# Two blocks on one core: where the second attention's latents are split, which of its values come first, and whether the last projection keeps its split weights

## The reference

```python
def second_block(x, positions, w_in, q_norm_g, w_uq, kv_norm_g, w_ukv, pool_w, pool_scale, w_out, ln_g, ln_b):
    alpha = (2.0 * DEPTH) ** 0.25
    h = x @ w_in
    x_q, x_kv, k_rope_raw, gate_a, u_pool, gate_b = jnp.split(h, splits, axis=-1)   # 512, 256, 64, 512, 512, 512
    y_a = mla_branch(x_q, x_kv, k_rope_raw, positions, q_norm_g, w_uq, kv_norm_g, w_ukv) * jax.nn.silu(gate_a)
    y_b = pool_branch(u_pool, pool_w, pool_scale) * jax.nn.silu(gate_b)
    mix = jnp.concatenate([y_a, y_b], axis=-1) @ w_out
    return layer_norm(alpha * x + mix, ln_g, ln_b)

def mla_branch(...):        # 4 heads, no causal limit in the work done: every block of 128 queries sees 1024 keys
    q = (rms_norm(x_q, q_norm_g) @ w_uq)                # 128 plain and 64 rotated columns a head
    kv = (rms_norm(x_kv, kv_norm_g) @ w_ukv)            # 128 key and 128 value columns a head
    # rope on q_rope and k_rope_raw, softmax(q k^T * scale, masked by position) @ v, in blocks of 128 queries
```

## Time and profile before

| | |
|---|---|
| median of 3 runs | 2448.18 us (2445.73 to 2453.65) |
| profiled execution | 2448.01 us |
| its span, first to last instruction | 2446.2 us |
| PE busy in the span | 2338.3 us (96%) |
| DVE, ACT, POOL busy | 1545.6, 781.1, 1145.2 us |
| input units of the second block end | 2057 us |
| attention, first logits to last values | 2153.9 to 2317.6 us |
| last projection | 2322.1 to 2425.5 us |

### The profile page before, as it was taken

How to read it: one execution, slowest core, us unless ns; L and a number is a source line. 1 busy time by engine, 2 the same in 40 slices (tenths; PEclk the granted TensorE clock), 3 DMA queues, 4 the chain that set the end, 5 groups by cost and what they waited for, 6 DMA issues and landing times. The chain is left out here.

```text
span 2446.2 us, 30442 instructions
## 1 busy us (share of the span) xinstructions
PE 2338.3 (96%) x11310; PEld 1931.9 (79%) x11310; DVE 1545.6 (63%) x1925; ACT 781.1 (32%) x1038; POOL 1145.2 (47%) x917
## 2 busy tenths in 40 slices
PE   7999999999999999999999999999999999899995
PEld 5678877888888898887778888788888877689874
DVE  7899999955556354445666667777777002434478
ACT  4311232133322356113333334334431122244413
POOL 4136523333222346433388888989864322200164
PEclk9999999999999999999999999999999999899998
DMA  4021224532222413444144445644412110411122
GB/s 153 31 85 61 77 86 129 163 119 92 100 95 87 129 36 118 137 133 155 69 174 163 146 143 219 232 159 152 147 44 82 43 43 22 146 48 40 49 77 95
DMA packets 97713, 261.51 MB, mean 107 GB/s; under 512 B 8304, under 2 KB 32120, under 8 KB 92600
## 3 DMA queue, kind: packets, MB, share of 16 engines
q1 hardware_dynamic: 79376, 192.77, 23.1%
q10 hardware_dynamic: 18216, 67.13, 7.9%
HBM read 183.57 MB, written 77.61 MB: 107 GB/s over the span
## 5 line engine op out<-in xcount | busy, mean ns | idle before, releaser
L998 PE MATMUL pair<-actA,w_hi 128*128 128x512 f32 x2048 | 638.0, 393 | 4.3 <-ACT stage L1532 2.3
L851 POOL TENSOR_TENSOR pad<-pad 128x1 f32<-128x1 f32 x142 | 39.2, 276 | 1059.4 <-PE pair L998 753.6
L998 PEld LDWEIGHTS pair<-actA,w_hi 128*128 128x128 f32 x2048 | 383.1, 188 | 88.1 <-issue 4.5
L998 PE MATMUL pair<-actA,w_lo 128*128 128x512 f32 x1024 | 399.3, 390 | 0.0
L855 POOL TENSOR_TENSOR w_lo<-raw,w_hi 128x1024 fp32r<-128x1024 f32 (+2 forms) x142 | 318.0, 2240 | 11.4
L1332 PE MATMUL pair<-tring,wsp 128*128 128x512 f32 x1344 | 308.4, 392 | 6.0 <-DVE tring L2529 5.7
L1332 PEld LDWEIGHTS pair<-tring,wsp 128*128 128x128 f32 x1344 | 254.1, 189 | 60.2 <-issue 6.5
L998 PEld LDWEIGHTS pair<-actA,w_lo 128*128 128x128 f32 x1024 | 192.6, 188 | 40.6
L1332 PE MATMUL pair<-tsp,wsp 128*128 128x512 f32 x768 | 184.5, 392 | 7.9 <-DVE u_c L2504 4.0
L2497 DVE TENSOR_TENSOR xB<-pair,xB 128x1024 f32<-128x1024 f32 x112 | 136.3, 1219 | 72.9 <-PE pair L1332 72.8
L998 PE MATMUL pair<-actB,w_hi 128*128 128x512 f32 x576 | 178.1, 390 | 0.0
(11 more groups left out here) (344 smaller groups left out, 4204.8 us busy)
## 6 DMA issues: line engine op xcount, KB each, us to landing
raw<-w_in SPq DMA_DIRECT2D x80, 512.0 KB, 3.3
wraw<-w_pair SPq DMA_DIRECT2D x32, 1024.0 KB, 7.1
staged<-hid_d SPq DMA_DIRECT2D x56, 512.0 KB, 3.3
proj<-stage ACTq DMA_DIRECT2D x40, 512.0 KB, 2.6
hid_d<-hsum SPq DMA_DIRECT2D x16, 1024.0 KB, 5.0
gates<-proj ACTq DMA_DIRECT2D x24, 512.0 KB, 5.3
raw<-w_out SPq DMA_DIRECT2D x24, 512.0 KB, 3.3
hid_d<-hid SPq DMA_DIRECT2D x16, 512.0 KB, 2.8
```

What stands on the lines that cost most here:

```text
L851: nc.gpsimd.tensor_tensor(pad[:, 0:1], pad[:, 1:2], pad[:, 1:2], ALU.add)
L998: last = nc.tensor.matmul(pair[par][:, cols], w[:, par, wk], x[:, cols], start=(k == 0 and i == 0), stop=(k == kt - 1 and i == 2))
```

## The change

Six edits, all in the second block:

1. ACT parks the residual `xB` in DRAM (`x_d`, two DMAs of 2 MB) after input unit 1; SP loads it back after it has issued the queries of attention block 2. Its 32 KB (and 112 to 120) hold six buffers for squares (`sq6`) and then the hi parts of the latents meanwhile. `xq_lo` takes 56 to 72 KB.
2. ACT squares x_q after input unit 13 and x_kv after unit 14; PE makes both means of squares after unit 15; ACT's roots and hi copies and DVE's norms and lo parts come before ACT reads units 16 and 17.
3. `swap(2)` (kr) follows the first unit of `w_uq`, `swap(0)` and `swap(1)` the second and the third; the rotary work of DVE and ACT moves forward with them. The four DMAs of the rotary queries are issued between the third and the fourth plain query unit.
4. The value heads come first in `w_ukv`, the key heads after them, and between key heads PE transposes the values and ACT copies them. The wait of attention for `k2` is per head.
5. The last projection has its own activation buffer `actC`, half by half: half 0's hi parts are made by ACT around its last two softmax steps, the lo parts by DVE between its last attention steps; half 1's follow the attention. Eight split weights are kept (`w_hi`/`w_lo`, `w_kept`, `w_last`), split once; half 1 splits none. Four half-wide PSUM banks take the products in turn in place of two.
6. POOL no longer centres and scales tiles 6 and 7 of half 1; DVE does all eight.

ACT's list between the second plain query unit and the key heads, before: `q2st` is a plain query head's buffer, `q_d` and `qr_d` DRAM, `k` the key heads.

The diff, cut:

```diff
-        xqS = at("xqS", 120, [P, 2, 4, S], F32R)
-        xkvS = at("xkvS", 152, [P, 2, 2, S], F32R)
-        tmp2 = at("tmp2", 168, [P, 2, S])
+        sq6 = at("sq6", 88, [P, 6, S])
+        xq_hi = at("xq_hi", 88, [P, 4, S], F32R)
+        xq_lo = at("xq_lo", 56, [P, 4, S], F32R)
+        xkv_hi = at("xkv_hi", 104, [P, 2, S], F32R)
+        xkv_lo = at("xkv_lo", 112, [P, 2, S], F32R)
+        rstd_kv = at("rstd_kv", 80, [P, S])
...
-        q2st = at("q2st", 56, [P, 2, 2, S], F32R)
+        q2st = at("q2st", 152, [P, 2, 2, S], F32R)
...
+        actC = at("actC", 120, [P, 2, NT, 2, HALF], F32R)
+        w_kept = [at(f"w_kept{j}", kb, [P, 2, 1024], F32R) for j, kb in enumerate((56, 64, 72, 80, 48))]
+        w_last = [at("w_last0", 195.5, [P, 1024], F32R), at("w_last1", 203.5, [P, 1024], F32R)]
...
+        def product_bank(c):
+            n = FIRST["out2"] + c
+            col = (c // 2) % 2 * HALF
+            return pair[n % 2][:, col:col + HALF]
...
             for b in range(NB):
                 load_q2(b)
+                if b == 2:
+                    sp.dma_start(xB[:, 0:4, :], x_d[:, 0:4, :]).then_inc(xB_back, 16)
+                    sp.dma_start(xB[:, 4:8, :], x_d[:, 4:8, :]).then_inc(xB_back, 16)
             load_units("w_out2", FIRST["out2"], NT, 8)
-            load_units("w_out2", FIRST["out2"] + NT, NT, 8)
...
-            split_units(FIRST["out2"], N_OUT2, 8)
...
+            for j in range(NT):
+                n = FIRST["out2"] + j
+                hi, lo = kept(j)
+                pool.wait_ge(w_in[n % 2], (n // 2 + 1) * 16)
+                if j < 2:
+                    pool.wait_ge(unit_mm, n - 1)
+                if j == 2:
+                    pool.wait_ge(unit_mm, FIRST["out2"] + 1)
+                if j == 6:
+                    pool.wait_ge(lo_ok, 4 * NT + 10 + 2 * NT)
+                nc.gpsimd.tensor_copy(hi, raw[:, n % 2, :]).then_inc(w_hi_ok, 1)
+                pool.wait_ge(w_hi_ok, n + 1)
+                nc.gpsimd.tensor_tensor(lo, raw[:, n % 2, :], hi.bitcast(F32), ALU.subtract).then_inc(w_split, 1)
...
+            product(n + 1, (n + 1) % 2, (n + 1) // 2, 8, hB, lB)
             stat("xq", "mean512", 4)
-            products(FIRST["in2"] + 15, 4, 8, hB, lB)
+            stat("xkv", "mean256", 2)
+            for n in range(FIRST["in2"] + 16, FIRST["in2"] + N_IN2):
+                product(n, n % 2, n // 2, 8, hB, lB)
...
-            stat("xkv", "mean256", 2)
...
+            swap(2)
             for u in range(1, N_UQ):
                 n = FIRST["uq"] + u
                 product(n, n % 2, n // 2, 4, qh, ql)
-                if u == 3:
-                    swap(0)
-                    swap(1)
-                if u == 4:
-                    swap(2)
+                if u <= 2:
+                    swap(u - 1)
             pe.wait_ge(lo_ok, base + 6)
-            products(FIRST["ukv"], N_UKV, 2, lambda k: xkvS[:, 0, k, :], lambda k: xkvS[:, 1, k, :])
...
+            for u in range(N_UKV):
+                n = FIRST["ukv"] + u
+                product(n, n % 2, n // 2, 2, lambda k: xkv_hi[:, k, :], lambda k: xkv_lo[:, k, :])
+                if u >= 4:
+                    unit_read(pe, n - 4)
+                    transposes(("v2T", u - 4), lambda c: v4[:, u - 4, c * P:(c + 1) * P], NB)
...
+                pe.wait_ge(unit_out[n % 2], n // 2 - (c >= 2))
...
+                if n == FIRST["in2"] + 2:
+                    for j in (0, 4):
+                        act.dma_start(x_d[:, j:j + 4, :], xB[:, j:j + 4, :]).then_inc(xB_out, 16)
...
                 nc.scalar.copy(q2st[:, h % 2, 0, :], pair[n % 2][:, :]).then_inc(q2_hi, 1)
                 n += 1
+                if h < 3:
+                    rope_hi(h)
                 if h >= 1:
                     park_q2(h - 1)
...
+                if h == 2:
+                    act.wait_ge(r_lo, 3)
                     for s in range(2):
                         rows = slice(s * 64, s * 64 + 64)
                         act.dma_start(qr_d[0:64, s::2, :], qr_hi[rows, :, :].bitcast(F32)).then_inc(qr_parked, 16)
                         act.dma_start(qr_d[64:128, s::2, :], qr_lo[rows, :, :].bitcast(F32)).then_inc(qr_parked, 16)
...
+            def first_half(i):
+                if i == N2 - 1:
+                    wait_ready(act, ("qk", 1, N2 - 1))
+                    branch_half(0, range(4))
+
+            attention(1, MLA_HEADS, at2, 0, first_half)
+            branch_half(0, range(4, NT))
             for b in (NB - 2, NB - 1):
                 wait_done(act, ("yT", 1, b))
+            branch_half(1, range(NT))
...
+            def first_half(i):
+                if i == N2:
+                    low_half(0, range(4))
+                if i == N2 + 2:
+                    low_half(0, range(4, NT))
+
+            attention(1, MLA_HEADS, P, float(192) ** -0.5, at2, 0, 0, mask2, gated, first_half)
             for b in (NB - 2, NB - 1):
                 wait_done(dve, ("yT", 1, b))
+            low_half(1, range(NT))
+            dve.wait_ge(xB_back, 32)
...
-            centre(1, mine[0:1])
+            centre(1, range(1))
             variance(1)
-            centre(1, mine[1:])
-            scale(1, mine)
+            centre(1, range(1, NT))
+            scale(1, range(NT))
```

More of the change, by code:

```diff
@@ L1428, in half_product @@
             def half_product(j, half):
[L1429 to L1439 removed]
+                c = half * NT + j
+                n, out = FIRST["out2"] + c, product_bank(c)
+                whi, wlo = kept(j)
+                if half == 0:
+                    pe.wait_ge(w_split, n + 1)
+                pe.wait_ge(unit_out[n % 2], n // 2 - (c >= 2))
+                for k in range(NT):
+                    if j == 0:
+                        pe.wait_ge(lo_ok, base + 6 + half * NT + k + 1)
+                    wk, xh, xl = slice(k * P, (k + 1) * P), actC[:, half, k, 0, :], actC[:, half, k, 1, :]
+                    for i, (w, x) in enumerate(((whi, xh), (whi, xl), (wlo, xh))):
+                        mm = nc.tensor.matmul(out, w[:, wk], x, start=(k == 0 and i == 0),
+                                              stop=(k == NT - 1 and i == 2))
                 mm.then_inc(unit_mm, 1)
@@ L1759, in _, with attention @@
                     square(STAT_BASE[("hg", h)], mpair(key)[:, :])
-            def attention(st, heads, buf, i0):
+            def attention(st, heads, buf, i0, beside=None):
                 N = NB * heads
                 for i in range(N + 1):
+                    if beside:
+                        beside(i)
                     if i < N:
@@ L2043, in finish @@
                 for j in tiles:
-                    if half and j in BY_POOL:
-                        act.wait_ge(scaled_pool, BY_POOL.index(j) + 1)
-                    else:
-                        act.wait_ge(scaled, NT * half + j - sum(x < j for x in BY_POOL if half) + 1)
+                    act.wait_ge(scaled, NT * half + j + 1)
                     nc.scalar.activation(xB[:, j, cols], xB[:, j, cols], ACT.Identity, bias=SM("ln_b", j),
@@ L2304, in _, with attention @@
             finish(HG_HEADS - 1)
-            def attention(st, heads, dv, scale, buf, i0, b0, mask, write):
+            def attention(st, heads, dv, scale, buf, i0, b0, mask, write, beside=None):
                 N = NB * heads
                 for i in range(N + 4):
+                    if beside:
+                        beside(i)
                     if i < N:
@@ L2718, in move @@
                 if j < 2:
-                    V.scalar_tensor_tensor(x, x, float(2.0 ** 0.25), pair[par][:, 0:HALF], ALU.mult, ALU.add) \
+                    V.scalar_tensor_tensor(x, x, float(2.0 ** 0.25), product, ALU.mult, ALU.add) \
                      .then_inc(unit_out[par], 1)
@@ L2722, in move @@
                     dve.wait_ge(lessened, half * (NT - 2) + j - 1)
-                    V.tensor_tensor(x, pair[par][:, 0:HALF], x, ALU.add).then_inc(unit_out[par], 1)
+                    V.tensor_tensor(x, product, x, ALU.add).then_inc(unit_out[par], 1)
                 dve.wait_ge(unit_out[par], n // 2 + 1)
@@ L2753, in gather_sq @@
                     V.tensor_tensor(sq_sum[:, cols], sq_sum[:, cols], sqh[:, c % 2, :], ALU.add).then_inc(dev_sum, 1)
-            mine = [j for j in range(NT) if j not in BY_POOL]
             def keep_mean(half):
@@ L2783, in gather_both @@
                 gather_sq(c)
-            move(0)
-            dve.wait_ge(lo_ok, base + NT)
+            dve.wait_ge(lo_ok, base + 2 * NT)
             for half in range(2):
                 c = half * NT
-                if half:
-                    move(c)
+                move(c)
                 move(c + 1)
```

173 lines of the change are left out of this document (83 added, 90 removed).

## The result

The changed kernel takes 2412.14 us (median of 4 runs, 2409.43 to 2413.58) against 2448.61 us of the kernel before, measured beside it: ratio 0.9848, 95% interval 0.9828 to 0.9867. Run again later it gave 2406.68 us (5 runs, 2405.63 to 2412.67), ratio 0.9831 (0.9817 to 0.9846). The forecast was 2412 us. The profiled execution took 2413.39 us, its span 2411.5, at a mean clock of 0.986.

What follows compares the result with a forecast made beforehand. PE bounds the kernel, busy 96% of the span, its late waits on DVE and ACT, never a DMA. Savings of 24.5 (to attention), 9.4 (last projection) and 2.4 (tail) sum to 36.3 us off 2448.01: 2412 us, range 2402 to 2422.

Steps and rivals of the forecast that it cites:

- signs of being wrong: Attention beginning later than 2135, PE waiting for `xB` in half 1, or block 3's queries landing late.
- Latents: Before `w_uq`: roots, norms, splits covered by three input units (32.7 us); first unit at 2058.4, no wait; parking and reload cost 0.
- Head units: `w_uq` to second value head: old waits go; ACT's four DMA issues (5.55 us) leave a 4.3 us wait plus 2.9 clock.
- Values first: Value and key heads: seven heads 19.0 us, transposes 4.0, nothing waits; attention starts at 2129.3, 24.5 us less.
- End of attention: Last attention steps: ACT's half-wide copies add 0.65 us; first half product at 2319.3, not 2322.11.
- First mean: After two half products: four DVE rests alternate with POOL's splits, 9.3 us; PE waits 4.9 us plus 2.9 of clock.
- Half 1: Last projection, second half: no split beside it, DVE's 30 to 34 us just hidden under 34 of PE, no waits.
- Tail: After the last product: DVE's seven centrings alone take 4.3 us, against five in 6.70 beside POOL; 2.4 us less.
- less waiting: Rival: DMA issues cost ACT little, or DVE isn't held before the first mean; 6 or 8 us less, 2404 to 2406; chance 0.2.
- the queue did not back up more: Rival, ACT's queue: rotary DMAs all at 2.41 us, 4 us, and 4 more before first value copy; 2416 to 2420; chance 0.17.
- DVE did not bound half 1: Rival, last projection: DVE's late start or waits add 3 to 10 us at the last product; 2415 to 2424; chance 0.1.
- block 3's queries: Slower rival: SP's 4 MB reload delays these queries and attention waits; 2457 if landing takes 85 us; chance 0.02.

Runs made afterwards that it cites:

- e9: The kernel before, run and profiled once more without any edit: first part 1998.55 us, 450.55 us behind the pooling.
- e5: Changed kernel with ACT's rotary-query DMAs and parks spread among the value reads: pooling to first logits 131.15 us against 133.33.
- e6: Changed kernel with POOL repeating eight weight splits beside half 1, in buffers nobody reads: tail 9.4 us longer, 10.6 in all behind the pooling.
- e7: Changed kernel with the half products in two PSUM banks, each waiting for the second before it: +4.3 us up to the last product.
- e4: Changed kernel with means of squares, roots and copies behind the last input unit, without cover: median 2414.95 us; middle 9.95 us longer.
- e1: Changed kernel with the four rotary-query DMAs issued by SP among its w_ukv loads instead of by ACT: 2414.76 us (4 runs).
- e11: Changed kernel with POOL's splits of reloaded branch halves two logits later in the first attention: median 2402.74 us, first part 1988.53 us.
- e8: Changed kernel with both POOL's repeated splits beside half 1 and two PSUM banks: 108.44 us to the last product, 15.1 us longer behind the pooling.
- e3: Changed kernel with POOL again centring and scaling tiles 6 and 7 of the last half: median 2409.55 us, tail 20.25 us, 2.45 more.

## Why the prediction was right, and where it was not

The time was met and the mechanisms were those forecast, but that it was met to a fraction of a microsecond is luck, since two errors cancel: the four parts gave 43.6 us and not 36.3, and the first window took 8.9 us back in the same execution. The second error is not the change's: e9 shows the long first window in the kernel before, and e5, e6 and e7 the short one with the change in. The 7.3 us of the first error lie in the middle (3.1), in attention and last projection together (3.6) and in the tail (0.5). The second profiles of both kernels (450.55 and 409.67 us behind the pooling) give 40.9 for the four parts. All runs of the two kernels together say 2448.69 (median of 48 runs) and 2410.62 (9 runs), 38.1 us.

One of the forecast's own signs of being wrong came: attention begins at 2135.11, later than 2135. It isn't the head units' doing, which are 3.1 us shorter than forecast, but the first window's 8.9 us; the sign was set in absolute time, as if that window were fixed. A slip of the forecast on which nothing rests: the 124 us left "from its last transposes" are counted from the first half product, and from the transposes they are 128.1.

- *Latents*: forecast was the first `w_uq` matmul 4.1 us sooner; it came 4.5 sooner (69.64 against 65.13 us behind the cut), without a wait. That the cover does it: e4. The parking cost nothing: 147.71 us from ACT's read of the first input unit to the cut with it and without, and its two DMAs lie in this stretch. Nobody waits for the reload; neither was tested by itself.
- *Head units*: the wait stood at the place forecast, behind the work forecast (5.6 us of issues for 5.55). It was 3.4 us, not 4.3. The step that failed is "first query head is parked at 2087.6": the DMA's issue has the start of the copy that stands two places ahead of it in ACT's list (2094.17 both, which is 2085.7 in the forecast's time), so the third head's copy never waited for the park. And of 2.9 us of clock behind the gap only some 1.5 came (0.71 in five us), worth less than that: in e6 and e7 the same 3.38 us gap kept full clock, PE then waited 0.6 to 0.7 us for ACT one head later, and the middle was only 0.3 to 0.4 us shorter. From first `w_uq` matmul to first logits 68.2 us, not 70.9. Together the middle gave 27.7 us for 24.5.
- *Values first*: no wait at any of seven units, as forecast. Edits 3 and 4 were not run apart, so which of them took away the old waits for the key heads (6.9 us) is argued and not shown.
- *End of attention*: +0.69 us for +0.65; first product 0.41 us behind the last transposes for 0.5. No run has the new last projection with the old late splits, so the price of the old 3.4 us wait for the first operand is read from the two timelines alone.
- *First mean*: the hold came turn and turn about, as forecast from the 2.83 us row, but the last four rests stood behind three operations of POOL and not four, 6.38 us for 9.3, since the first of them got in as POOL's first began. Wait 1.84 for 4.9. The 2.9 us of clock didn't come in this profile, but 1.6 to 1.9 came in e1, e6, e7 and e11. Last product 93.66 us behind the transposes for 97.2. That is 3.5 us less where wait and clock are 6.0 less; part of the difference is a term mis-sized the other way, the three means between the halves, 2.5 us (2357.99 to 2360.49) for the 1.3 forecast.
- *Half 1*: without waits, as forecast; why before had them: e6 to e8.
- *Tail*: 2.9 for 2.4; e3 shows 2.45 of it, the other half a microsecond I did not trace.
- *Rivals*: "less waiting" is what the profile behind the pooling shows (some 7 us more), hidden by the first window; the queue did not back up more; DVE did not bound half 1; block 3's queries were issued at 2168.86 behind the reload and nobody waited for them.

What was missing is a term for the clock's chance: I took a gap's price (2.9 us for 4.93) from one row as a fixed sum, and the untouched three quarters of the span as fixed too. In e9 the same gap cost 1.2 us less.

## What to carry to other kernels

Cut both spans at shared events before crediting a change: the parts showed 2.45 us in the tail where the medians had the other sign. A row of DMAs in an engine's list is worth its issue time to the first instruction behind it, and moving it gains only what its new queue doesn't hold back: 5.0 us lost behind SP, 2.2 won when spread. More PSUM banks let PE run ahead of a slow engine, but most of the delay then comes where the backlog must be gone: 10.3 us of waits at the products with two banks (e8), 9.5 behind the last product with four (e6).

## What the runs showed that I had not expected

- The clock behind a gap of PE is not a function of the gap alone: 1.86 to 1.99 us at one place kept full clock in four profiles and lost it in two; 1.84 or 1.85 us at the first mean kept it in six profiles (among them both of the changed kernel) and lost it in four (e1, e6, e7 and e11, 0.66 in five us each); 3.38 us at the second value head kept it in e6 and e7 and lost it in the others that have it (0.66 to 0.72). The Trainium skill, "TensorE: Matmul & The Clock Gate", "Part 1: The HAM clock gate (the "warmup" mystery)", calls the number of matmuls at the lower clock run-variable at a kernel's start; these rows show the same late in a long one: with the same gap PE runs at the lower clock in some executions and not in others.
- A reload that came 1.2 us late in the first attention was followed by 6.2 us of loss on PE; but e9 is 4.1 us behind at the same place without a late reload (1.91 us of gap), so most of it is the clock's.
- Four DMAs of 512 KB issued back to back by one engine took it 0.53, 0.63, 1.89 and 2.42 us, two parks of 1 MB behind them 4.98 together; spread over 11 us, 0.53, 0.62, 0.52, 2.29, 2.35 and 2.60. The same instruction held the engine for 0.5 or for 2.4 us. That what is still in the queue decides this fits the order of the numbers, but no run tests it.
